# Identity transposes on the tensor engine between its start and the first four token tiles of a one-core decoder layer

## What is computed

```python
h = x * rsqrt(mean(x * x) + EPS) * g      # RMSNorm of each token
z = h @ w_in                              # columns: q, k, v, u, v_sg, gate_a, gate_b
...                                       # attention, spatial gating, merge, w_out, SwiGLU
```

## Time and profile before

| what | value |
|---|---|
| median of 3 runs | 1619.86 us (1619.34 to 1619.95) |
| the profiled execution's own time | 1618.66 us |
| its span | 1616.9 us |
| PE busy | 1565.0 us, 97% of the span |
| DVE busy | 542.4 us, 34% |
| ACT busy | 494.5 us, 31% |
| GpSimd busy | 149.5 us, 9% |
| mean granted clock of PE | 0.984 of full speed |

### The profile page before, as it was taken

One profiled execution on the slowest core, in us unless ns is written; L12 is line 12 of the kernel. 1 busy time (PEld: TensorE's weight loads), 2 busy tenths in 40 slices (PEclk: granted clock), 3 DMA queues, 4 the chain that ended last, 5 costly groups with the idle time before them and its releaser, 6 DMA issues.

```text
span 1616.9 us, 23673 instructions
## 1 busy us (share of the span) xinstructions
PE 1565.0 (97%) x9929; PEld 1520.2 (94%) x9929; DVE 542.4 (34%) x1006; ACT 494.5 (31%) x953; POOL 149.5 (9%) x188
## 2 busy tenths in 40 slices
PE   5999999999999999999999999999999999999995
PEld 5999999899999998998789999999999999999995
DVE  6104550332013354274653131132123113212236
ACT  5215543442224422144773202211211121121123
POOL 1000000000000036050001100100110110010014
PEclk9999999999999999699999999999999999999998
DMA  6111112001102035015422111111111111111102
GB/s 196 41 51 40 40 55 80 27 28 40 40 27 82 27 85 172 27 53 185 154 82 79 49 53 40 53 49 44 49 44 54 40 53 40 54 40 53 40 26 105
DMA packets 127557, 100.80 MB, mean 62 GB/s; under 512 B 4888, under 2 KB 114464, under 8 KB 127456
## 3 DMA queue, kind: packets, MB, share of 16 engines
q1 hardware_dynamic: 124208, 91.67, 18.2%
q0 software_dynamic: 3104, 7.11, 1.5%
q10 hardware_dynamic: 144, 0.52, 0.1%
HBM read 91.56 MB, written 7.73 MB: 61 GB/s over the span
## 4 chain that ended last, share of the span: by engine, by line
PE 89%; DVE 4%; ACT 2%; DMA 1%; issue 1%; POOL 1%; DVEq 0%; ACTq 0%
PE bank L892 29%; PE bank L472 11%; PE bank L474 10%; PE bank L473 10%; PE bank L900 5%; PE bank L902 5%; PE bank L901 5%; PE psT L468 3%; PE psB L807 1%; PE psC L659 1%; PE bank L862 1%; PE bank L861 1%; PE bank L860 1%; PE psA L659 1%; DMA qb<-q_rows 1%
## 5 line engine op out<-in xcount | busy, mean ns | idle before, releaser
L892 PE MATMUL bank<-f_hi,w_hi 128*128 128x384 f32 (+1 forms) x1056 | 339.2, 321 | 5.9 <-issue 3.3
L892 PE MATMUL bank<-f_hi,w_lo 128*128 128x384 f32 (+1 forms) x1056 | 337.8, 320 | 0.0
L892 PE MATMUL bank<-f_lo,w_hi 128*128 128x384 f32 (+1 forms) x1056 | 337.4, 320 | 0.0
L472 PE MATMUL bank<-h_hi,w_hi 128*128 128x344 f32 x1008 | 335.6, 333 | 1.6 <-DVE h_lo L1509 1.4
L1496 DVE TENSOR_TENSOR w_lo<-w_raw,w_hi 128x1024 fp32r<-128x1024 f32 x138 | 169.0, 1225 | 472.9 <-ACT w_hi L1420 230.8
L474 PE MATMUL bank<-h_hi,w_lo 128*128 128x344 f32 x1008 | 324.5, 322 | 0.0
L473 PE MATMUL bank<-h_lo,w_hi 128*128 128x344 f32 x1008 | 324.3, 322 | 0.0
L892 PEld LDWEIGHTS bank<-f_hi,w_hi 128*128 128x128 f32 x1056 | 198.5, 188 | 7.7 <-issue 3.9
L892 PEld LDWEIGHTS bank<-f_lo,w_hi 128*128 128x128 f32 x1056 | 198.5, 188 | 0.0
L892 PEld LDWEIGHTS bank<-f_hi,w_lo 128*128 128x128 f32 x1056 | 198.5, 188 | 0.0
L472 PEld LDWEIGHTS bank<-h_hi,w_hi 128*128 128x128 f32 x1008 | 192.0, 190 | 5.9 <-issue 4.6
(11 more groups left out here) (398 smaller groups left out, 1894.2 us busy)
## 6 DMA issues: line engine op xcount, KB each, us to landing
w_raw<-in_w_in SPq DMA_DIRECT2D x42, 512.0 KB, 3.9
w_raw<-in_w_out SPq DMA_DIRECT2D x24, 512.0 KB, 3.6
w_raw<-in_w_gate SPq DMA_DIRECT2D x23, 512.0 KB, 3.9
w_raw<-in_w_up SPq DMA_DIRECT2D x23, 512.0 KB, 3.9
w_raw<-in_w_down SPq DMA_DIRECT2D x22, 512.0 KB, 3.5
xin<-in_x_prompt SPq DMA_DIRECT2D x8, 512.0 KB, 7.6
xn<-in_x_prompt SPq DMA_DIRECT2D x8, 512.0 KB, 4.9
out_y_prompt<-xn SPq DMA_DIRECT2D x8, 512.0 KB
```

What stands on the lines that cost most here:

```text
L472: mm(out[:, 0:TG], w_hi[par][:, ws], hi[:, k, tgc[tg]], start=first, stop=False)
L892: ins = mm(out[:, 0:NG[tg]], w[par][:, ws], x[tg][:, k, :], start=(k == 0 and w is w_hi and x is f_hi), stop=(k == KD - 1 and w is w_lo))
```

## The change

Before each of the first four tiles, ahead of the wait for the scaled tile, PE issues a number of further transposes: 40 before tile 0, 8 before tile 1, 12 before tile 2 and 8 before tile 3. Each takes `ident` as its data and writes columns 0 to 127 of `psC`. None waits for anything or raises a semaphore. Nothing else is changed.

```diff
                 t = step
                 src, rows = (xin[t], P) if t < 8 else (xins, NS)
+
+                for _ in range((40, 8, 12, 8)[t] if t < 4 else 0):
+                    turn(psC[:, 0:P], ident[:, :])
                 pe.wait_ge(x_h, t + 1)
                 if t >= 2:
                     pe.wait_ge(x_lo, t - 1)
```

## The result

The changed kernel takes 1632.79 us (median of 7 runs, 1628.61 to 1638.52), the kernel before 1618.6 us in the same comparison (7 runs, 1614.25 to 1619.95). The ratio is 1.0093 with a 95% interval of 1.0078 to 1.0109: slower by about 15 us. The profiled execution of the change has a span of 1630.7 us against 1616.9.

The account below looks back on a forecast made before the run. PE, busy 97% of the span, was taken as the bound. Job "a" at full clock (1.44 us) and beginning earlier (0.2 us) sum to 1.65 us, giving 1618.2 us against the median of 1619.86; range 1617.3 to 1620.5.

Parts of the forecast that it names:

- The step on the transposes themselves: In the start: fetching the 136 added instructions costs nothing, or if uncovered, single stalls of tenths of a microsecond.
- other: Anywhere in the kernel: remaining causes, such as instruction stream stalls, to either side; no size given, chance 0.04.
- same: Whole kernel: a difference within what the measurement can tell, about 0.2% or 3.2 us; chance 0.93.
- The 40: Before tile 0: the transposes end at 7.8 us, or 10.3 all at half clock, before the tile at 11.42; no cost.
- The terms of job "a": Job "a" in the start: full clock saves 1.44 us (5.29 to 3.85), and an earlier beginning saves 0.2 us.
- rival 4: Job "a": its clock state may vary between runs by itself, so no gain; lower end of Rival 1's 0.43.
- Rival 1: Hole before tile 3: the clock falls again, job "a" begins slow, 0.5 us gain left, 1619.4 us; chance 0.43.
- Rival 2: Tiles 0 to 3: added transposes don't raise the clock and delay job "a" by 1.8 us, 1621.7 us; chance 0.04.
- Rival 3: 640.5 to 674 us: the clock holds through the hole at 637 us, saving 17 us, 1601 us; chance 0.04.

Follow-up runs that it names:

- 128 transposes: 68, 8, 26 and 26 transposes before tiles 0 to 3, against the kernel before: 1617.7 us against 1618.79, ratio 0.9994.
- 34: Half of the change, 20, 4, 6 and 4 transposes before tiles 0 to 3, added to the kernel before: 1618.9 us in one run.
- 76: 42, 8, 12 and 14 transposes before tiles 0 to 3, against the kernel before: 1614.01 us against 1614.63, ratio 0.9986.
- 90: 54, 8, 16 and 12 transposes before tiles 0 to 3, added to the kernel before: 1617.41 us in one run.
- the three runs without transposes in the start: Transposes added elsewhere to the kernel before: 68 behind job "f" (1622.66 us), 68 behind the feed-forward loop (1629.06 us), 67 behind job "f" (1640.83 us).
- 67 and 68: 67 or 68 transposes behind job "f" instead of in the start, added to the kernel before: 1640.83 us against 1622.66.
- 68 and 69 in the start: The change, and the change with one more transpose before tile 0 (41, 8, 12, 8): 1632.79 us, and 1612.37 us, ratio 0.9971 to the kernel before.
- the run with 60: 36, 8, 10 and 6 transposes before tiles 0 to 3, added to the kernel before: 1625.82 us in one run.

## Why the prediction was wrong, point by point

**What failed.** The step on the transposes themselves: "68 transposes are 136 instructions, whose fetch I cost at nothing, covered by the idle time before 11.42; uncovered, single stalls of the order of tenths of a microsecond". That looked only at the fetch of the new instructions where they stand. What they cost is the fetch of others, 1100 us later: 17.1 us, at jumps whose holes went from 3.3 to 13.1 us in all and took the clock with them. The three holes of 1.1 us put down to "issue" were in the waits of the kernel before; they were the sign that the loop does not stay loaded, and I did not take them as a term. None of the rivals held this mechanism; "other", which names stalls of the instruction stream, had 0.04 and no price. Nor does any run show the added "tenths of a microsecond": the one other entry "issue" of PE, 0.2 us at L472, is in the kernel before too, and the waits for code at the jumps are 1 us and more. The 0.93 for "same" earns nothing: the slowdown of 0.9% is clear of its interval, and it is "same" only by a bound as wide as 2%.

The range was too narrow apart from that. It allowed 0.6 us of scatter to either side, from four executions within 1.3 us; the later runs of the kernel before spread over 8 us (1613.13 to 1621.38).

**What held in the start.** The 40 ended at 8.3 us (7.8 forecast), the transposes of tiles 0 to 3 ran at full clock, ACT and DVE got nothing earlier or later, and job "a" waited for DVE. The terms of job "a" were right where the clock held: with 128 transposes 3.84 us (3.85 forecast), job "c" 1.72 us earlier (1.65 forecast), still 1.72 us at 485 us (of which part may be the scatter of the kernel before, see rival 4); with 34, 76 and 90 it was 3.84 to 3.85 us too.

**Rival 1 came true** in the profile of the change: the clock fell at 23 us after the hole of 2.28 us. Whether it falls is not settled by the length of that hole alone: it fell after 2.16, 2.28 and 2.55 us and held after 0.23, 1.59, 1.84 and 2.68, and in the changed kernel it held after the 3.00 us before tile 0, which the prediction took as likely to cost it. So what decides is open, and each profile is only one execution. **Rival 4** has something to it: in the three runs without transposes in the start, job "c" began at 35.40, 35.29 and 36.21 us, where the kernel before had 35.85, so the start scatters by 0.9 us untouched.

**Rival 2 did not occur.** Transposes of the identity raised the clock: in the changed kernel the first 21 of the 40 started 0.21 us apart, up to 5.93 us, and the others 0.11 us apart, with nothing else on PE. The Trainium skill, TensorE: Matmul & The Clock Gate, section Part 4: PE-mode transpose, says that the full clock does not engage for transposes; for these float32 ones the spacing decides against it.

**Rival 3** rested on a wrong reading. In the changed kernel the hole before the cached values was absent, PE was busy throughout, and the clock fell all the same, at 637.4 us (0.71 over the microsecond from 637), and stayed at half until past 671. Windows of PE in the changed kernel:
```profile
637.00:638.00 1.00, 1.00 (x7) 0.97 (x7) 0.00 (x0) 0.00 (x0) 0.00 (x0) 0.71 1.09 324
638.00:671.00 33.00, 33.00 (x133) 32.03 (x133) 1.16 (x3) 1.58 (x3) 0.00 (x0) 0.50 0.01 4
```
So the half clock goes with this stretch, in which the two-column matmuls stand, and does not need the hole ahead of it. No run took these matmuls out.

**What is shown and what is argued.** Shown: the holes, the length of the branch and the number of instruction loads depend on where the loop begins, with a period of one block (128 transposes), with a jump in price between two neighbouring places (67 and 68, and 68 and 69 in the start), and with the edge found at the counted instruction in three kernels (1, 2 and 17 instructions ahead of it). Shown too: with the loop at 0 to 15 behind an edge nothing is loaded at the jumps, elsewhere nine blocks are loaded for each pass. Argued: that the reason is seven blocks against eight, that is, how many blocks stay loaded. No run had a shorter or longer loop. The Trainium skill, Runtime: NRT & Kernel Launch, section Instruction fetch mechanics, gives PE 128 KiB of instruction memory, 2048 instructions, refilled in blocks of 16 KiB, and says that the sequencer fetches the next block while it executes the current one. By that, as an estimate, seven blocks and one fetched ahead fit, and eight and one don't; the seven loads of the first pass, none after it, and nine for each pass of a loop over eight blocks agree. The same section also says that a taken branch waits for a fetch if its target is not in the current window of two pages, and a loop of seven blocks that loads nothing at its jumps does not agree with that.

## What to carry to other kernels

Added instructions can cost more than their own time when a long loop stands behind them: look at the holes "issue" behind the jumps of every loop, and at the count of instruction loads, before and after. If a loop's code spans seven blocks from an edge on, as here, shift its start to just behind an edge (69 instead of 68 transposes: a ratio of 0.9971 instead of 1.0093), and don't leave it just ahead of one. Compare the stretch that holds the loop and not only the whole time, which scattered by more than the gain. Keeping the clock up in the start was worth 1.7 us here at most, and no median showed it.

## What was not expected of the hardware

A jump back in a loop over seven blocks of code left no hole (its branch took 0.21 us), over eight it left one of 1.0 to 1.5 us (the branch took 3.3 to 3.8 us, most of it covered by matmuls already issued), and of 4.0 to 4.5 us when the target was the last or the last but one instruction of its block. In the run with 60, PE went on 1.1 us after the last matmul ahead of the jump, and had the second block at 3.9 us; where both were needed at once, the hole was about as long as the latter. A 4.5 us hole cost about 2.4 us more behind it (7.3 us for three): at the first jump the clock came back only at about 1115 us, almost 5 us after work had begun again at 1110.4.
